# A hybrid decoder layer with retrieved experts: 144 tokens gathered instead of 128, and the dense v products with the tokens as columns

## What is computed

```python
q = (xt @ w_q).reshape(T, PEER_HEADS, 2, PEER_DHALF)
s = jnp.einsum('thcd,hcnd->thcn', q, sub_keys)
...                                      # top 16 of each half, top 16 of their sums: eidx, gates
a = jnp.einsum('td,ted->te', xs, u[es])  # 128 experts of each token
hact = jax.nn.gelu(a) * gs
return jnp.einsum('te,ted->td', hact, v[es])
```

## Time and profile before

| | us |
|---|---|
| median of 3 runs | 3590.52 (3590.32 to 3590.65) |
| the profiled execution | 3590.52 |
| its span in the profile | 3588.7 |
| expert stage, first dense product to last | 1462.4 to 3581.2 |

### The profile page before, as it was taken

The page is one execution under the profiler, slowest core; times in us unless marked ns, Lnnn a source line. Parts: engine busy times, 40 slices in busy tenths (PEclk is TensorE's granted clock), DMA queues, the critical chain, the costliest instruction groups (busy, mean ns, idle before and its releaser), DMA issues.

```text
span 3588.7 us, 51464 instructions
## 1 busy us (share of the span) xinstructions
PE 3360.4 (94%) x16926; PEld 2943.4 (82%) x16926; DVE 2234.7 (62%) x3867; ACT 1124.8 (31%) x1743; POOL 1158.9 (32%) x870
## 2 busy tenths in 40 slices
PE   7999999677989957899999999999999999999999
PEld 5778876566868746799899899999998998998998
DVE  2003312695026989677777777767777777777776
ACT  3122223443222239523322222232223233222222
POOL 2344431163435520232332322323333333333322
PEclk9999999798999979999999999999999999999999
DMA  4233320002332204888788888877888887888886
GB/s 139 76 88 94 94 82 15 1 1 101 99 105 83 71 35 187 293 270 267 260 272 265 266 267 267 269 265 261 275 262 265 268 266 261 270 265 265 268 266 232
DMA packets 276020, 686.84 MB, mean 191 GB/s; under 512 B 120544, under 2 KB 120800, under 8 KB 273504
## 3 DMA queue, kind: packets, MB, share of 16 engines
q1 hardware_dynamic: 202224, 417.51, 36.0%
q0 software_dynamic: 73728, 268.47, 22.2%
HBM read 655.48 MB, written 30.41 MB: 191 GB/s over the span
## 4 chain that ended last, share of the span: by engine, by line
PE 59%; ACT 2%; issue 1%; DMA 1%; DVE 0%; ACTq 0%; DVEq 0%; SPq 0%
PE exp_a L1866 10%; PE exp_a L1868 10%; PE exp_a L1867 10%; PE exp_o L1887 10%; PE exp_o L1889 10%; PE exp_o L1885 10%; ACT table_gaps L1684 1%; ACT table_stage L1700 1%; DMA gate_table<-table_stage 0%; PE table_b L1644 0%; DMA exp_raw<-in_v 0%; DVE table_hot L1670 0%; ACTq L1684 0%; ACTq L1700 0%; PE table_t L1635 0%
## 5 line engine op out<-in xcount | busy, mean ns | idle before, releaser
L1866 PE MATMUL exp_a<-x_high,exp_uh 128*128 128x384 f32 x2048 | 685.9, 335 | 11.6 <-DVE exp_ul L1950 11.6
L1868 PE MATMUL exp_a<-x_high,exp_ul 128*128 128x384 f32 x2048 | 685.7, 335 | 0.0
L1867 PE MATMUL exp_a<-x_low,exp_uh 128*128 128x384 f32 x2048 | 685.4, 335 | 0.0
L1889 PE MATMUL exp_o<-exp_vh,exp_al 128*128 128x512 f32 x1536 | 598.2, 389 | 0.0
L1887 PE MATMUL exp_o<-exp_vl,exp_ah 128*128 128x512 f32 x1536 | 598.1, 389 | 0.0
L1885 PE MATMUL exp_o<-exp_vh,exp_ah 128*128 128x512 f32 x1536 | 597.5, 389 | 0.0
L1845 POOL DMA_INDIRECT exp_rows<-in_v_rows,exp_now x256 | 323.6, 1264 | 712.2 <-DVE h L1971 653.7
L1845 POOL DMA_INDIRECT exp_rows<-in_u_rows,exp_now x256 | 298.7, 1167 | 734.2 <-DVE exp_rows L1964 689.2
L1915 ACT CAST exp_vh<-exp_raw 128x1024 fp32r<-128x1024 f32 x256 | 260.1, 1051 | 516.7 <-PE exp_o L1889 493.3
L1950 DVE TENSOR_TENSOR exp_vl<-exp_raw,exp_vh 128x1024 fp32r<-128x1024 f32 x256 | 304.6, 1220 | 166.6 <-ACT exp_vh L1915 165.5
L1866 PEld LDWEIGHTS exp_a<-x_high,exp_uh 128*128 128x128 f32 x2048 | 385.6, 188 | 13.2 <-DVE exp_ul L1950 7.5
(11 more groups left out here) (292 smaller groups left out, 5194.7 us busy)
## 6 DMA issues: line engine op xcount, KB each, us to landing
exp_raw<-in_u SPq DMA_DIRECT2D x256, 512.0 KB
exp_raw<-in_v SPq DMA_DIRECT2D x256, 512.0 KB
w_in_raw<-in_w_in SPq DMA_DIRECT2D x88, 512.0 KB, 3.6
gate_table<-table_stage SPq DMA_DIRECT2D x6, 4096.0 KB, 11.6
exp_gates<-gate_table SPq DMA_DIRECT2D x128, 192.0 KB
w_out_raw<-in_w_out SPq DMA_DIRECT2D x32, 512.0 KB, 3.6
w_q_raw<-in_w_q SPq DMA_DIRECT2D x32, 512.0 KB, 3.8
x_rows<-in_x SPq DMA_DIRECT2D x4, 1024.0 KB, 8.1
```

The source lines that it names most:

```text
L1866: pe.matmul(bank, uh[:, b, c, :], xh[:, 0:DENSE_TB, c, :], start=(c == 0), stop=False)
L1867: pe.matmul(bank, uh[:, b, c, :], xl[:, 0:DENSE_TB, c, :], start=False, stop=False)
L1868: last = pe.matmul(bank, ul[:, b, c, :], xh[:, 0:DENSE_TB, c, :], start=False, stop=(c == DC - 1))
L1889: last = pe.matmul(bank[:, :], al[:, key, tokens], vh[:, dc % 2, key, :], start=False, stop=(key == KEYS_OF_MACRO - 1))
```

## The change

The first 368 tokens (`DENSE_RUNS = 23` runs of `RUN = 16`, `TD` = 368) are computed densely. The last 128 are gathered as before. The 16 between them are gathered too, but spread over the partitions: eight partitions (`SHARES`) hold a copy of each of these tokens, and each of the eight does 16 of its 128 picks. So there are 16 more picks of 128 rows, two tasks a macro (both in step 0, ahead of the other two), 18 tasks in all.

The v products are turned round: 128 output elements of v are the weights, the 368 columns are tokens. A v step of 512 elements is four units (`BLOCKS`) of one bank each, 16 units a macro, in a ring of six banks. The result is transposed (elements on partitions), so the sums no longer go into `h`: they go into a new tile `sums` (16 x 368 a partition), which POOL clears during the table stage. The residual is written to HBM (`h_rows`) during the second norm and read back at the end; there PE transposes the 16 units back and DVE adds them. The shared tokens' partial sums are folded by four products with a selection matrix in the last macro.

The transposed tokens are stored in runs of 16 (`[P, RUNS, DC, RUN]` instead of `[P, TB, DC, P]`). The table's sixth part has 48 tokens, stored by a DMA of its own shape. Order of work on the engines is otherwise kept.

```diff
-DENSE_TB = 3
-TD = DENSE_TB * P
+DENSE_RUNS = 23
+TD = DENSE_RUNS * RUN
...
 # gate_table, SP
-            with sp.Fori(0, PARTS // 2) as q:
-                for s in range(2):
-                    sp.wait_ge(banks_out, q * (2 * slots_of_part) + (slots_of_part * (s + 1) + SLOTS))
-                    sp.dma_start(table[q * 2 + s], stages[s][:]).then_inc(stored[s], 16)
+            for q in range(PARTS):
+                tokens = tokens_of(q)
+                sp.wait_ge(banks_out, slots_of_part * q + tokens // SLOT_TOKENS + SLOTS)
+                sp.dma_start(table[q][:, :, 0:tokens], stages[q % 2][:, :, 0:tokens]).then_inc(stored[q % 2], 16)
...
 # experts
-TASKS = 2 * STEPS_OF_MACRO
+TASKS = 2 * STEPS_OF_MACRO + 2
+BLOCKS = PC // P
+UNITS = D // P
+RING = 6
...
 # PE, u_step
-                    pe.matmul(bank, uh[:, b, c, :], xh[:, 0:DENSE_TB, c, :], start=(c == 0), stop=False)
+                    pe.matmul(bank, uh[:, b, c, :], xh[:, 0:DENSE_RUNS, c, :], start=(c == 0), stop=False)
...
 # PE, v_step
-                for key in range(KEYS_OF_MACRO):
-                    if key % 2 == 0:
-                        pe.wait_ge(low, m * CHUNKS + (chunk + key // 2))
-                    if dc == 0:
-                        pe.wait_ge(a_split, m * KEYS_OF_MACRO + (key + 1))
-                    for tb in range(DENSE_TB):
-                        bank = o_bank[dc % 2 * DENSE_TB + tb]
-                        tokens = slice(tb * P, (tb + 1) * P)
-                        if key == 0:
-                            wait(pe, o_out, m * units + (dc * DENSE_TB + tb + 1 - 2 * DENSE_TB))
-                        pe.matmul(bank[:, :], ah[:, key, tokens], vh[:, dc % 2, key, :],
-                                  start=(key == 0), stop=False)
+                for half in range(2):
+                    pe.wait_ge(low, m * CHUNKS + (chunk + half))
+                    for b in range(BLOCKS):
+                        unit = dc * BLOCKS + b
+                        bank = o_bank[unit % RING]
+                        if half == 0:
+                            freed = unit - RING if unit >= RING else unit - (4 if unit < 4 else 10)
+                            wait(pe, o_out, m * UNITS + (freed + 1))
+                        for key in (2 * half, 2 * half + 1):
+                            if unit == 0:
+                                pe.wait_ge(a_split, m * KEYS_OF_MACRO + (key + 1))
+                            pe.matmul(bank[:, 0:TD], vh[:, dc % 2, key, column(b)], ah[:, key, :],
+                                      start=(key == 0), stop=False)
...
+                        if half:
                             last.then_inc(o_done, 1)
...
 # ACT, split_high
-                        wait(act, o_done, m * units + (split[1] - 1) * DENSE_TB)
+                        wait(act, o_done, m * UNITS + (split[1] - 1) * BLOCKS)
...
 # DVE
             def add_out(m, dc):
-                for tb in range(DENSE_TB):
-                    dve.wait_ge(o_done, m * units + (dc * DENSE_TB + tb + 1))
-                    sums = h[:, tb, dc * PC:(dc + 1) * PC]
-                    dve.tensor_tensor(sums, sums, o_bank[dc % 2 * DENSE_TB + tb][:, :], ALU.add)\
+                for b in range(BLOCKS):
+                    unit = dc * BLOCKS + b
+                    dve.wait_ge(o_done, m * UNITS + (unit + 1))
+                    dve.tensor_tensor(sums[:, unit, :], sums[:, unit, :], o_bank[unit % RING][:, 0:TD], ALU.add)\
                         .then_inc(o_out, 1)
...
+            def add_back(unit):
+
+                dve.wait_ge(returned, unit + 1)
+                bank = a_bank[unit % 2][:, 0:DENSE_TB * P].rearrange("p (b d) -> p b d", d=P)
+                cols = back_rows[:, 0:DENSE_TB - 1, column(unit)]
+                dve.tensor_tensor(cols, cols, bank[:, 0:DENSE_TB - 1, :], ALU.add)
+                cols = back_rows[0:EXTRA, DENSE_TB - 1, column(unit)]
+                dve.tensor_tensor(cols, cols, bank[0:EXTRA, DENSE_TB - 1, :], ALU.add).then_inc(return_out, 1)
...
                     if step > KEYS_OF_MACRO:
-                        add_out(m, step - 1 - KEYS_OF_MACRO)
-                    elif step == 0 and not (isinstance(m, int) and m == 0):
-                        add_out(m - 1, D // PC - 1)
-                    task(m, kind, 2 * step)
-                    task(m, kind, 2 * step + 1)
+                        dc = step - 1 - KEYS_OF_MACRO
+                        add_out(m, dc)
...
+                    elif step == 0:
+                        if not (isinstance(m, int) and m == 0):
+                            add_out(m - 1, D // PC - 1)
+                        task(m, pair, odd, kind, 0)
+                        task(m, pair, odd, kind, 1)
+                    task(m, pair, odd, kind, 2 * step + 2)
+                    task(m, pair, odd, kind, 2 * step + 3)
...
 # build, SP and POOL in the second norm
+        sp.dma_start(h_rows.rearrange("(b p) d -> p b d", p=P), h[:, :, :]).then_inc(h_kept, 16)
+        pool.tensor_tensor(gain_row[:], scaled_rows[:, TB - 2, :], gain_row[:], ALU.mult).then_inc(plain_ready, 1)
```

More of the change, by code:

```diff
@@ L170, in _ @@
                 act.wait_ge(turned, c + 1)
[L171 removed]
+                act.activation(columns(hi, c), grouped(banks[c % NORM_BANKS]), ACT.Copy,
                                scale=gain[:, c:c + 1]).then_inc(high, 1)
@@ L1718, with experts @@
 SPLITS = (("v", 0), ("u", 2), ("u", 3), ("v", 1), ("u", 4), ("v", 2), ("v", 3), ("u", 5))
-def experts(nc, place, h, xT, raw, loaded, loads, table, table_stored, out, sparse):
+BLOCKS = PC // P
+UNITS = D // P
+RING = 6
+def experts(nc, place, h_rows, xT, raw, loaded, loads, table, table_stored, out, sparse):
     xh, xl = xT
@@ L1823, in _ @@
                 sp.wait_ge(s, 16 * PARTS // 2)
-            run(sp, macro)
-            columns = out.rearrange("(b p) d -> p b d", p=P)
+            run(sp, macro, between)
+            sp.wait_ge(a_done, MACROS * KEYS_OF_MACRO)
+            sp.dma_start(extra_rows[:, :], h_rows[TD:T - P, :]).then_inc(back_in, 16)
+            sp.dma_start(back_rows[:, :, :], h_rows[0:T - P, :].rearrange("(b p) d -> p b d", p=P))\
+                .then_inc(back_in, 16)
+            columns = out[0:T - P, :].rearrange("(b p) d -> p b d", p=P)
@@ L1834, in _, with gather @@
+            sp.wait_ge(stored, 16 * (2 * (D // PC) + 2))
         @block.gpsimd
         def _(pool):
-            def macro(m, kind):
-                for t in range(TASKS):
-                    slot, turn, place_now = t % ROW_SLOTS, t // (2 * NOW), t // 2 % NOW
-                    if t % (2 * NOW) == 0:
+            def gather(m, pair, odd, kind, t, index):
+                slot = slot_of(odd, t)
+                wait(pool, task_done, m * TASKS + (t - ROW_SLOTS + 1))
+                pool.sem_inc(waited, 1)
+                pool.indirect_dma_start(
+                    rows[slot][:, :], None, sparse["u" if kind == "dot" else "v"],
+                    bass.IndirectOffsetOnAxis(ap=index, axis=0),
+                    element_offset=t % 2 * (NK * NK * HALF_D)).then_inc(rows_in[slot], 16)
@@ new lines, in macro @@
+            def macro(m, pair, odd, kind):
+                pool.tensor_copy(now_shared[:, :], sparse["shared_experts"][:, pl(shared_pick(m, kind), 1)])\
+                    .then_inc(now_ready, 1)
+                pool.wait_ge(now_ready, m * 3 + 1)
+                for t in range(2):
+                    gather(m, pair, odd, kind, t, now_shared[:, 0:1])
+                for t in range(2, TASKS):
+                    turn, place_now = (t - 2) // (2 * NOW), (t - 2) // 2 % NOW
+                    if (t - 2) % (2 * NOW) == 0:
@@ L1850, in _ @@
+                    gather(m, pair, odd, kind, t, now[:, turn, place_now:place_now + 1])
             run(pool, macro)
@@ L1894, in macro @@
-            def macro(m, kind):
+                for half in range(2):
[11 more added lines that the diff above has]
+                                      start=(key == 0), stop=False)
+                            pe.matmul(bank[:, 0:TD], vh[:, dc % 2, key, column(b)], al[:, key, :],
+                                      start=False, stop=False)
+                            last = pe.matmul(bank[:, 0:TD], vl[:, dc % 2, key, column(b)], ah[:, key, :],
+                                             start=False, stop=(key == KEYS_OF_MACRO - 1))
+                        if half:
+                            last.then_inc(o_done, 1)
@@ new lines, in fold, with give_back @@
+            def fold(n):
+                if n == 0:
+                    pe.wait_ge(task_done, end * TASKS + 2)
+                if n < 2:
+                    pe.wait_ge(gelu_done, end * KEYS_OF_MACRO + (n + 3))
+                else:
+                    pe.wait_ge(fold_out, n - 1)
+                pe.matmul(a_bank[n % 2][0:RUN, :], sparse["selection"][:, :],
+                          shared_sums[:, n * PC:(n + 1) * PC], start=True, stop=True).then_inc(folded, 1)
+            def give_back(unit):
```

(11 more changed lines are left out.)

244 lines of the change are left out of this document (174 added, 70 removed).

## The result

The changed kernel takes **3786.0 us** (median of 4, 3785.4 to 3789.1) against 3590.4 for the kernel before: ratio **1.0547** (95% interval 1.0534 to 1.056). It is slower by 195.5 us. The forecast was 3719 us, slower by 129, with a range up to 3790: the sign and the main mechanism were right, the sum was 67 us short, and the result lies only 4 us inside the range. The profiled execution has a span of 3787.2 us, 198.5 more than before.

What follows compares the result with a forecast made beforehand. TensorE (PE), busy 94%, was taken to bound the kernel, never waiting in the expert stage. 3590.5 - 61.4 + 144 + 27 - 5.6 + 10 + 2 + 13 = 3719.5 us, range 3675 to 3790.

Steps and rivals of the forecast that it cites:

- fewer columns: Expert stage: 368-column products take 166.7 ns each, a macro 64.07 us against 65.99; -61.4 us in 32 macros.
- short runs: u products and products for the queries: pieces in runs of 16 tokens cost PE nothing; 0 us.
- two ring waits a macro: Second and third v steps: PE waits about 2.2 us each for DVE's addition to free a bank; +144 us.
- clock: Expert stage: one ring wait in four loses PE's clock, 1.7 us each; +27 us, ends 0 and 109.
- table: one iteration, and POOL's clearing: Gate table stage: 23 iterations in place of 24, -5.6 us; POOL's clearing of the sums is covered by the stage.
- narrow store: Last table store: runs of 192 bytes take about 23 us against 12.7, all on the path; +10 us.
- middle and end: DVE's extra work between macros +2 us; last macro's folds and returns and additions behind the last matmul together +13.
- The rival in which the ring never bites: Expert stage: no ring waits and no clock loss, everything else stays; 3549 us, chance 4%.
- The rival that I gave 7%, one column a piece: u products and products for the queries: each short piece costs a column, +60 us; 3780 us, chance 7%.
- the rival in which it falls at every wait (10%): Expert stage: PE's clock falls at all 64 ring waits, 109 us in place of 27; 3802 us, chance 10%.
- Norm, DVE, gathers: Residual store and POOL's second row product in the norm, DVE's two more tasks and added gathers a macro cost 0.
- The rival of a late gather: Expert stage: DVE or a gather becomes late as well, another 1 us a macro, +32; 3752 us, chance 7%.

Runs made afterwards that it cites:

- e9: e8 with queries reading one piece and the 368 dense columns copied through HBM into their own tile, so u products read one piece: 3578.5 us, ratio 0.9969.
- e8: Changed kernel with the order of e1, the whole store of e4 and POOL's clearing of the sums in 16 pieces: 3590.4 us, ratio 0.9994.
- e2: Changed kernel with the additions of units 0 and 1 ahead of the split in step 5 alone: 3683.0 us, ratio 1.026.
- e4: Changed kernel with the last part of the table stored whole, 16 unused tokens with it: 3781.1 us, ratio 1.0537.
- e1: Changed kernel with DVE's additions of units 0 and 1 of a v step moved ahead of the split in steps 5, 6 and 7: 3600.6 us, ratio 1.0035.
- e5: Kernel before the change with only the transposed tokens in runs of 16, a u product reading 24 pieces instead of 3: 3642.1 us, ratio 1.0147.
- e6: Kernel before the change with only the transposed tokens in runs of 32, 12 pieces instead of 3: 3613.9 us, one execution.

## Why the prediction was right or wrong

| term | forecast, us | measured, us | read from |
|---|---|---|---|
| fewer columns, 32 macros | -61.4 | -61.4 + 25 | v steps of 8.09 us; 168.9 ns in e9 |
| short runs | 0 | +28 | 0.87 x 32, e8 against e9 |
| two ring waits a macro | +144 | +140 | (2.22 + 2.29) x 31; e2 shows 2.29 |
| clock | +27 | +46 | 1.53 x 30 |
| table: one iteration, and POOL's clearing | -5.6 | -2.5 | 3.1 of it from e8 |
| narrow store | +10 | +9 | first macro of e4 |
| middle and end | +15 | +14 | 6.7 in the last macro's v steps, 7.7 behind the last product |

**The ring: right.** The step that carried the forecast, an addition that stands behind the split of the next chunks while its bank is wanted one v step sooner, held in place (units 6 and 10, none in the first and fourth v step), in count (62 where 64 were forecast, the last macro having none) and in size. From the starts above it is 3.75 - 1.53 + 2.29 = 4.51 us a macro against 4.5. e1 takes it away by order alone. The rival in which the ring never bites (3549 us) is refuted.

**Short runs: wrong.** This is the largest miss, 28 us. The step took the 13.3 ns that are over with one piece and with three to say that a piece has no price, and carried this to 23 pieces. It holds for long pieces: the products for the queries before read four pieces of 128 columns and stand 227 ns apart (1111.44 to 1119.83 us, 37 products), as the v products with one piece of 512 do. It doesn't hold for runs of 64 bytes. The rival that I gave 7%, one column a piece, is what e5 and e6 show at 384 columns. In the changed kernel a u product takes 173.4 ns, and 168.9 in one piece (e9): there the 22 more pieces cost 4.5 ns, 0.20 each, half of what they cost at 384 columns, and why is open. The Trainium skill ("Advanced Engine Details and Errata", SBUF Cachelines) wants two hits on each 16-byte line, which runs of 64 bytes fulfil; the measurement disagrees (182.5 against 173.3 ns with nothing else changed) and decides.

**Columns: the size was off, 25 us.** The v products have one piece and take 168.5 ns, not 166.7, and u products in one piece (e9) take 168.9. The line through 384 and 512 columns doesn't go on down to 368. A cause that suggests itself is the weight load. Over 1000 us of e9 the loads are busy without a gap; but so they are in a u stage of the kernel before, where 384 columns pay the same 13.3 ns as 512:

```profile
2500.00:3500.00 1000.00, 1000.00 (x5932) 1000.00 (x5931) 797.26 (x911) 291.99 (x368) 405.28 (x325) 1.00 0.86 288
```
```profile
2525.61:2558.90 33.29, 33.29 (x193) 33.28 (x192) 23.45 (x25) 8.84 (x13) 8.13 (x9) 1.00 0.84 274
```

So these rows don't decide it, and no run has the weights loaded at another rate: the cause stays open.

**The clock: mechanism right, count wrong.** One wait in four was to lose it; 30 of the 31 first waits of a macro did (1.96 us of idle time), and no second one (2.04 us), so the rival in which it falls at every wait (10%) came half true. A loss costs 1.53 us and not 1.7, since at the lower level the products stand 0.307 us apart, which is 368 columns at 1.2 GHz with nothing over: the 13 ns on top of the columns are only there at the upper level. The two rows (1.94 us without a loss, 2.00 with one) couldn't give a count; I took a number between and it was low. Why the first wait and not the second, and why 7 of 31 in e2, where the wait is as long, stays open.

**Table stage.** The narrow store was forecast at 23 us and took 24.9, and the added term of 10 is near the 9 that e4 shows in the first macro. The price came from short reads of another queue, so this is agreement with a bound rather than a proof. The Trainium skill ("DMA: Bandwidth & Descriptors", Specifications) warns of a read-modify-write below 512 bytes; with the doubling that the forecast considered beside it the store would have taken an estimated 44 us, and it took 24.9. POOL's clearing was costed at nothing under the cover of 24 iterations. It had the time, but it held DVE for 3.1 us ahead of the first of them, on the path: the cover was named for the duration and not for who else was held.

**Norm, DVE, gathers: right at 0.** The second norm didn't become longer, POOL's second row product is hidden. DVE waits for gathers now and then (46.1 us in 22 waits for rows of v, 23.4 in 21 for rows of u), but this reaches PE nowhere in the waits above. The rival of a late gather didn't come.

**The end** was forecast at 10.5 us of DVE's work behind the last product, and DVE ends 11.1 us behind the start of that product. The whole got longer by 7.7 and not by the 8.5 that were added, as the program ends 4.1 us behind DVE's last operation where before it was 6.4. In the last macro the folds and first returns cost 6.7 us where 4 were forecast.

The measured terms sum to about 198, against 198.6 between the profiled spans and 195.5 between the medians. Of the 69 us by which the forecast fell short of the spans, 28 are the runs, 25 the columns, 19 the clock and 3 POOL's clearing; 6 for the ring, the store and the end go the other way. That the result still fell inside the range is in part luck: the range left room for part of the runs' price, for a late gather that didn't come and for a clock lost more often, and not for the columns.

## What to carry to other kernels

When a loop is cut into more units than its ring has banks, look at where the step that frees a bank stands in its engine's order: here a ring that covered a whole step before became two units too short, and moving two additions ahead of a split was worth 185 us, over 5%, at no cost in work. A layout chosen to make columns fewer can cost as much as it saves: 16 fewer columns saved 4.4 ns a u product as long as it read one piece (173.3 to 168.9 in e9), and the 23 runs took all of it back (173.4). Price an engine's idle time by its length as well as its sum, since a 2 us stretch can cost 1.5 us of clock on top and two of 1 us cost none.

## What the runs showed of the hardware

- A moving operand in short runs slows an fp32r matmul of 384 columns: 173.3, 177.8, 182.5 and 209.4 ns for 3, 12, 24 and 48 runs of 512, 128, 64 and 32 bytes.
- The runs' price was 16 ns at 512 columns with 32 runs of 64 bytes (243 against 227), none with 4 runs of 512 bytes (227, as with one piece), and 4.5 ns at 368 columns with 23 (173.4 against 168.9).
- PE idle for 1.0 us never cost the clock (62 waits), for 2.0 us it did in 7 of 31 when there was one a macro, and with two a macro at the first in 30 of 31 and at the second in none. Each loss was 3.4 us at 0.50.
- One POOL memset of 5888 f32 a partition (5.00 us) held a DVE copy of 0.23 us until its own end (4.83 us), with two operations behind it. Sixteen memsets of 368 did not.
- A store from SBUF to HBM of 16,384 runs of 192 bytes took 24.9 us, the same tile whole, in rows of 32 KB a partition, 12.7.
- With 368 columns the distance between matmuls was 168.4 to 168.9 ns, and not the 166.7 of the line through 384 and 512.
